# Second block's mixing stage: half of the RWKV mix ahead of the key ranking, half gates moved, key squares and first values on ScalarE

## What is computed

```
h = rms_norm(x)
cols_a, cols_b, gate_a, gate_b = split(h @ w_in)
cols = cols_a + (token_shift(cols_a) - cols_a) * mu     # the RWKV mix; token_shift moves rows down by one
r, k, v, wd, ad, gd = split(cols)                       # 512, 512, 512, 64, 64, 128 columns
a, g = sigmoid(a0 + ad @ a2), sigmoid(gd) @ g2
v_first = v  (layer 0)   or   v = v + (v_first - v) * sigmoid(v0 + (v @ v1) @ v2)  (layer 1)
kk = heads(k * k_k);  kk = kk / max(sqrt(sum(kk * kk)), 1e-12)      # 8 heads of 64
y_a = rwkv7_scan(r, decay, k, v, -kk, kk * a)  (then normed, and times g)
y_b = attention over the 64 keys that rank highest by an index score, from cols_b
x = x + (sigmoid(gate_a) * (y_a @ w_a) + sigmoid(gate_b) * (y_b @ w_b)) @ w_out
```

## Time and profile before

| what | value |
|---|---|
| median of 3 runs | 2837.88 us (2837.84 to 2838.81) |
| profiled execution | 2834.33 us, its span 2832.2 us |
| PE busy | 2696.9 us (95%) |
| DVE busy | 1518.7 us (54%) |
| ACT busy | 1051.0 us (37%) |
| POOL busy | 144.5 us (5%) |
| mean granted TensorE clock | 0.984 |

### The profile page before, as it was taken

The page is one execution under the profiler, slowest core; times in us unless marked ns, Lnnn a source line. Parts: engine busy times, 40 slices in busy tenths (PEclk is TensorE's granted clock), DMA queues, the critical chain, the costliest instruction groups (busy, mean ns, idle before and its releaser), DMA issues.

```text
span 2832.2 us, 35062 instructions
## 1 busy us (share of the span) xinstructions
PE 2696.9 (95%) x15034; PEld 2016.6 (71%) x15034; DVE 1518.7 (54%) x1662; ACT 1051.0 (37%) x1223; POOL 144.5 (5%) x117
## 2 busy tenths in 40 slices
PE   9999999999999999998899999988899899999998
PEld 7886687887878686886565468875564588785477
DVE  5455536455454535456773354457743457564367
ACT  4433434434443333433320144433201245454255
POOL 0002000000021000001011000010110000000000
PEclk9999999999999999998999999999999899999999
DMA  6654235656553254653422435545214167577786
GB/s 238 218 188 149 75 134 193 214 185 218 185 176 131 90 179 157 207 174 139 159 84 75 151 134 206 180 154 159 91 61 148 30 223 265 203 244 246 260 282 230
DMA packets 227470, 483.98 MB, mean 171 GB/s; under 512 B 11676, under 2 KB 45084, under 8 KB 227124
## 3 DMA queue, kind: packets, MB, share of 16 engines
q1 hardware_dynamic: 227316, 481.75, 49.3%
HBM read 477.01 MB, written 2.95 MB: 169 GB/s over the span
## 4 chain that ended last, share of the span: by engine, by line
PE 83%; DVE 11%; ACT 2%; DMA 2%; issue 2%; SPq 0%; POOL 0%; DVEq 0%; POOLq 0%; ACTq 0%
PE psum L424 17%; PE psum L426 17%; PE psum L425 17%; PE psum L427 15%; PE psum L471 4%; DVE weight_ring_low_halves L419 3%; PE psum L3162 2%; PE psum L2301 2%; PE psum L579 2%; PE psum L2387 1%; PE psum L988 1%; ACT weight_high_halves L413 1%; PE psum L681 1%; DMA weight_ring<-in_w_in 1%; PE psum L3092 1%
## 5 line engine op out<-in xcount | busy, mean ns | idle before, releaser
L419 DVE TENSOR_TENSOR weight_ring_low_halves<-weight_ring,weight_high_halves 128x2048 fp32r<-128x2048 f32 (+3 forms) x310 | 684.1, 2211 | 632.7 <-ACT weight_high_halves L413 632.4
L424 PE MATMUL psum<-weight_high_halves,stage_area_halves 128*128 128x512 f32 (+3 forms) x2150 | 827.1, 385 | 20.9 <-ACT stage_area L560 10.0
L426 PE MATMUL psum<-weight_high_halves,stage_area_halves 128*128 128x512 f32 (+3 forms) x2150 | 812.6, 378 | 0.0
L413 ACT ACTIVATE weight_high_halves<-weight_ring 128x2048 fp32r<-128x2048 f32 (+2 forms) x323 | 595.5, 1848 | 565.8 <-PE psum L426 244.8
L425 PE MATMUL psum<-weight_ring_low_halves,stage_area_halves 128*128 128x512 f32 (+2 forms) x1930 | 727.4, 377 | 0.0
L424 PEld LDWEIGHTS psum<-weight_high_halves,stage_area_halves 128*128 128x128 f32 x2150 | 406.5, 189 | 142.0 <-issue 46.1
L427 PE MATMUL psum<-weight_ring,stage_area 128*128 128x512 f32 x1088 | 475.0, 595 | 5.8 <-issue 5.8
L426 PEld LDWEIGHTS psum<-weight_high_halves,stage_area_halves 128*128 128x128 f32 x2150 | 406.4, 189 | 79.7
L425 PEld LDWEIGHTS psum<-weight_ring_low_halves,stage_area_halves 128*128 128x128 f32 x1930 | 364.7, 189 | 68.5 <-issue 0.2
L427 PEld LDWEIGHTS psum<-weight_ring,stage_area 128*128 128x128 f32 x1088 | 205.1, 191 | 257.8 <-issue 257.5
L560 ACT ACTIVATE stage_area<-psum 128x512 f32<-128x512 f32 (+3 forms) x134 | 73.6, 559 | 474.8 <-PE psum L426 148.5
(11 more groups left out here) (312 smaller groups left out, 2455.4 us busy)
## 6 DMA issues: line engine op xcount, KB each, us to landing
weight_ring<-in_ffn_w_gate SPq DMA_DIRECT2D x44, 1024.0 KB, 5.1
weight_ring<-in_ffn_w_up SPq DMA_DIRECT2D x44, 1024.0 KB, 5.2
weight_ring<-in_ffn_w_down SPq DMA_DIRECT2D x44, 1024.0 KB, 5.0
weight_ring<-in_w_in SPq DMA_DIRECT2D x36, 1024.0 KB, 5.3
weight_ring<-in_moe_wd SPq DMA_DIRECT2D x27, 1024.0 KB, 5.0
weight_ring<-in_moe_wu SPq DMA_DIRECT2D x25, 1024.0 KB, 7.1
weight_ring<-in_moe_wg SPq DMA_DIRECT2D x22, 1024.0 KB, 6.1
weight_ring<-in_mem_w_kv SPq DMA_DIRECT2D x16, 1024.0 KB, 5.3
```

Source lines behind the costliest of these rows:

```text
L413: act.raw.activation(self.high_half(name), self.in_slot(name), ACT.Copy).then_inc(*act.mark("high_halves", ("high", name)))
L419: v.raw.tensor_tensor(self.low_half(name), self.in_slot(name), self.high_half(name), ALU.subtract).then_inc(*v.mark("low_halves", ("halves ...
L424: pe.raw.matmul(out, a[1], w[0], start=start, stop=False)
L426: return pe.raw.matmul(out, a[0], w[0], start=False, stop=stop)
```

## The change

The mix is cut in two. Columns of r and k (`mix_first`) are mixed before DVE copies the turned heads, the rest (`mix_rest`) after the attention as before. The DMAs for the shifted r and k rows, and their part of mu, stand in the stream right behind the pieces of `colsA`, ahead of gate (0, 0)'s, and wait for the first two column blocks alone. Both zero rows are cleared by POOL. One row tile of gate (0, 1) is multiplied ahead of the attention, in both layers, and in layer 1 one row tile of gate (1, 1) ahead of the operands' turn; the other row tiles stay where the whole gates were. The squares of kk and their sums move to ACT, as 16 instructions of 64 columns, behind the second sigmoid and ahead of the copies of g; the copy of layer 0's first values moves to ACT behind these copies. The eight parameter rows of RWKV are loaded when the last values are multiplied instead of when they are copied.

```
-        order = [(b, m) for b in range(len(pr["cols"])) for m in range(MT)]
+        order = [(b, m) for b in range(len(pr["cols"])) for m in rows]
...
+        self.mu_rk, self.mu = net.part(12288, D), net.part(18688, N_A - D)
...
             st["a_in"] = net.plan_proj(f"rwkv{l}_in", w[:, 0:N_A], blocks(N_A), KT, split=True)
+            taken = [(st["a_in"]["tag"], "out", b, m) for b in range(2) for m in range(MT)] + self.turn_need(("mix", l))[0] + self.turn_need(("mix", l))[1]
+            net.load_param(("mu_rk", l), self.mu_rk, row_broadcast(ins["rwkv_mu_2"][l][0:D], D), [("x", x0 + 3 * l, 1)])
+            self.load_shifted(l, 0, taken)
...
-            net.load_param(("vec", l, j), self.vec[:, j, :], src, [(f"dsa{l}", "oT", 1)], topic="loaded_rwkv_vectors")
+            net.load_param(("vec", l, j), self.vec[:, j, :], src, [(f"dsa{l}", "weighted", 3)], topic="loaded_rwkv_vectors")
...
+    def zero_gpsimd(self, pool, l, i, taken):
+
+        pool.wait_ge(*pool.at(*taken))
+        pool.raw.memset(self.shifted[i][1][0:1, 0, :], 0.0).then_inc(*pool.mark("zero_row_ready", ("zero_row", l, i)))
...
+    def mix_vector(self, v, l, i):
+        v.wait_ge(*v.at(("loaded", ("shift", l, i, 2)), ("loaded", ("mu" if i else "mu_rk", l)), ("zero_row", l, i)))
+        for event, cols, B, mu in self.mix_rest if i else self.mix_first:
...
         act.raw.activation(self.a, self.a, ACT.Sigmoid).then_inc(*act.mark("rate_sigmoid", ("a", l)))
+        self.key_squares_scalar(act, l)
         for m in range(MT):
             act.wait_ge(*act.at(("wag", l, 2, m)))
...
+        else:
+            act.raw.activation(net.vfirst[:, :].rearrange("p (m n) -> p m n", m=MT), self.v, ACT.Copy).then_inc(*act.mark("first_values_kept", "vfirst"))
...
+    def key_squares_scalar(self, act, l):
+
+        act.wait_ge(*act.at(("keys_scaled", l)))
+        for m in range(MT):
+            for h in range(8):
+                part = slice(h * HD, (h + 1) * HD)
+                inst = act.raw.activation(self.squares[:, m, part], self.kk[:, m, part], ACT.Square, accum_out=self.hs[:, 8 * m + h:8 * m + h + 1])
+        inst.then_inc(*act.mark("keys_squared", ("key_squares", l)))
...
         v.raw.tensor_tensor(self.bh, self.r, self.k, ALU.mult).then_inc(*v.step())
         v.wait_ge(*v.last)
+        v.wait_ge(*v.at(("key_squares", l)))
...
             self.gate_tensor(pe, l, 0, 0)
+            self.gate_tensor(pe, l, 0, 1, [0])
             pairs_tensor(net, pe, f"dsa{l}", self.dsa_heads(l), self.dsa_pairs)
 
-            self.gate_tensor(pe, l, 0, 1)
+            self.gate_tensor(pe, l, 0, 1, [1])
...
             self.gate_tensor(pe, l, 1, 0)
+            self.gate_tensor(pe, l, 1, 1, [0] if l else [])
             net.turn_tensor(pe, self.operand_turn(l))
             self.solve_tensor(pe, l)
             self.chunks_tensor(pe, l)
 
-            self.gate_tensor(pe, l, 1, 1)
+            self.gate_tensor(pe, l, 1, 1, [1] if l else range(MT))
...
             net.split_vector(v, pieces[12:])
+            self.mix_vector(v, l, 0)
             net.turn_copy(v, self.dsa_turn(l))
-            v.wait_ge(*v.at(*net.proj_names(st["a_in"])))
-            v.raw.memset(self.shifted[0][1][0:1, 0, :], 0.0)
-            v.raw.memset(self.shifted[1][1][0:1, 0, :], 0.0).then_inc(*v.mark("zero_row_ready", ("zero_row", l)))
...
-            self.mix_vector(v, l)
+            self.mix_vector(v, l, 1)
```

More of the change, by code:

```diff
@@ L472, in passes, with proj_tensor @@
                 yield i, k, mm
-    def proj_tensor(self, pe, pr, lhsT, bank, need=(), turn_1=(), rows_first=False, before_last=(), before=(None, ())):
+    def proj_tensor(self, pe, pr, lhsT, bank, need=(), turn_1=(), rows_first=False, before_last=(), before=(None, ()), rows=range(MT)):
         tag, kts = pr["tag"], pr["kts"]
         halves = kts // 4
-        order = [(b, m) for b in range(len(pr["cols"])) for m in range(MT)]
+        order = [(b, m) for b in range(len(pr["cols"])) for m in rows]
         if turn_1:
@@ L1765, in __init__ @@
         self.at, self.bh, self.tmp = rows(17408), rows(18432), rows(19456)
+        self.squares = by_m(net.ax_buf[:, 0:D])
         self.vT, self.vv = net.part(17408, 4, S), net.part(20480, S)
@@ L1825, in __init__ @@
                 if (nb, j) == (0, 1):
[L1826 to L1831, removed]
+                    self.load_shifted(l, 1, net.proj_names(st["a_in"]))
+                    net.load_param(("mu", l), self.mu, row_broadcast(ins["rwkv_mu_2"][l][D:N_A], N_A - D), [("dsaT", l, "k")])
                 if (nb, j) == (1, 1):
@@ L1860, in __init__, with load_shifted @@
             self.layers.append(st)
+    def load_shifted(self, l, i, taken):
+        net = self.net
+        cols, to = self.shifted[i]
+        topic = ("loaded_shifted_keys", "loaded_shifted_rest")[i]
+        net.load_param(("shift", l, i, 0), to[1:113], self.colsA[0:112, :, cols], taken, topic=topic)
+        net.load_param(("shift", l, i, 1), to[113:P], self.colsA[112:P - 1, :, cols], topic=topic)
+        net.load_param(("shift", l, i, 2), to[0:1, 1, :], self.colsA[P - 1:P, 0, cols], topic=topic)
     def load_vectors(self, l):
@@ L2183, in prepare_vector @@
         v.wait_ge(*v.at(("loaded", ("vec", l, 7))))
-        v.raw.tensor_tensor(self.kk, self.k, row(2), ALU.mult).then_inc(*v.step())
-        v.wait_ge(*v.last)
+        v.raw.tensor_tensor(self.kk, self.k, row(2), ALU.mult).then_inc(*v.mark("keys_times_factor", ("keys_scaled", l)))
         net.turn_copy(v, self.low_rank_turn(l)[1:])
-        if l == 0:
-            self.key_squares_vector(v, l)
         for j, dst in ((0, self.sig), (1, self.a)):
@@ L2223, in prepare_vector @@
             v.raw.tensor_tensor(self.v, self.v, self.bh, ALU.add).then_inc(*v.step())
-            v.wait_ge(*v.last)
-        else:
-            v.raw.tensor_copy(net.vfirst[:, :].rearrange("p (m n) -> p m n", m=MT), self.v).then_inc(*v.step())
             v.wait_ge(*v.last)
@@ L2553, in gate_bank, with gate_tensor @@
         return 2 if (nb, j) == (0, 0) else 6
-    def gate_tensor(self, pe, l, nb, j):
+    def gate_tensor(self, pe, l, nb, j, rows=range(MT)):
         net = self.net
@@ L2558, in gate_tensor, with gate_scalar @@
         net.proj_tensor(pe, self.layers[l]["gates"][nb, j], lambda k, m: net.xT[:, k, m * P:(m + 1) * P],
-                        lambda b, m: self.gate_bank(nb, j) + m, joined)
-    def gate_scalar(self, act, l, nb, j):
+                        lambda b, m: self.gate_bank(nb, j) + m, joined, rows=rows)
+    def gate_scalar(self, act, l, nb, j, rows=range(MT)):
         net, tag = self.net, self.layers[l]["gates"][nb, j]["tag"]
-        for m in range(MT):
+        for m in rows:
             bank = self.gate_bank(nb, j) + m
@@ L2857, in gpsimd @@
             self.join_gpsimd(pool, l)
+            self.zero_gpsimd(pool, l, 0, [])
             rstd(("dsa", l), 0, 18)
             rstd(("dsai", l), 20, 2)
+            self.zero_gpsimd(pool, l, 1, self.net.proj_names(self.layers[l]["a_in"]))
             rstd(("kk", l), 0, 16)
```

26 lines of the change are left out of this document (9 added, 17 removed).

## The result

| | before | after | ratio |
|---|---|---|---|
| first comparison, four runs each | 2837.86 us (2834.83 to 2838.81) | 2822.34 us (2818.59 to 2828.09) | 0.9946 [0.9931, 0.9962] |
| repeat, on one chip | 2837.56 us (25 runs) | 2827.47 us (6 runs) | 0.9963 [0.9949, 0.9978] |
| second repeat, on another | 2835.91 us (23 runs) | 2827.70 us (12 runs) | 0.9967 [0.9955, 0.9978] |
| all 22 runs after, 87 before | 2837.4 us (2828.4 to 2843.7) | 2827.4 us (2818.6 to 2832.1) | |

Single executions of one kernel lie up to 15 us apart, and their time goes largely with the mean granted clock of TensorE (before: 2829.7 us at 0.985, 2842.2 at 0.981).

What follows compares the result with a forecast made beforehand. PE was taken to bound the kernel (83% of the chain). Terms -0.8 - 8.85 - 1.0 = -10.65 us took the profiled 2834.33 to 2823.7; with 3.55 for the median, 2827.2 us, range 2823.0 to 2833.0.

Steps and rivals of the forecast that it cites:

- more is gained: Rival: ACT's sums cost under 0.37 us each and the clock stays up, giving 2824.2 us; chance 0.15.
- Mix of r and k: Ahead of DVE's turned-head copies: layer 0 hides it at no cost; layer 1's index scores come 0.8 us later.
- The parameter rows: Loads beside the attention's end: between 0 and 2 us late for kk, taken as 0.
- Half ahead of the attention: Half of gate (0, 1) fills PE's pause before the attention: 2.5 us gained in layer 0, 1.7 in layer 1.
- 1.0 for the clock: First turns in both layers: shorter PE idleness may keep the clock up, 0 to 2.3 us together, taken as 1.0.
- Layer 0 behind the attention: Operands' turn starts at 1447.8 instead of 1448.59 us, as ACT's sums give back the earlier start: -0.8 us.
- The row against ScalarE: Squares and sums take DVE 2.5 us, ACT 5.9; leaving them on DVE would gain 1.7 us more in layer 0.
- Layer 1 behind the attention: Operands' turn at full speed saves 2.45 us, half a gate gone behind the scan 7.0; together -8.85 with 0.6 later start.
- Late rows: Rival: shifted rows five us late in both layers delay index and gates, giving 2832.4 us; chance 0.09.
- a loss from the sums on ACT: Rival: each of 16 sums takes 1.06 us, both layers lose, giving 2844.4 us; chance 0.05.
- it does nothing: Rival: the halves push out attention and turn by as much as they save behind; time stays; chance 0.03.
- The clock doesn't follow: Rival: PE stays slow in the pairs and the turn, 1.0 + 2.45 us are missing, giving 2830.7 us; chance 0.11.

Runs made afterwards that it cites:

- g11_whole: The changed kernel with gate (1, 1) whole again behind the scan in both layers; 2826.70 us.
- mix_before: The changed kernel with the mix of r and k back behind the attention and its rows loaded there; 2833.67 us.
- after_again: The changed kernel once more, unedited, giving its third profile; 2827.70 us, ratio 0.9967 to before.
- only_turn: The changed kernel with all undone but layer 1's half of gate (1, 1), the early loads and zero rows on POOL; 2830.91 us, ratio 0.9980 to before.
- halves_whole: The changed kernel with gates (0, 1) and (1, 1) both whole again; 2831.94 us, ratio 0.9986 to before.
- g01_whole: The changed kernel with gate (0, 1) whole again behind the attention in both layers; 2831.85 us.

## Why the prediction was right or wrong

**The sum came out, the range did not.** The sum of -10.65 us met 22 runs after and 87 before at -10.0; that it came out so near is partly luck, as its terms below miss in opposite directions. The step that failed is the one from the profiled execution to the median, with the range around it: the runs' own error was taken as half a microsecond or so, because three runs of before lay within 1 us, and the 3.55 us between the median and the profiled execution were carried over as a constant. The runs scatter by 13 to 15 us, and the profiled execution of after was the highest of its first four: not 3.55 below the median but 5.8 above it (0.2 above and 2.8 below in the two repeats). Of medians of four taken from the 22 runs, 95% lie between 2821 and 2831, so the range needed some 2 us more below, and even then 2822.3 is near its end. The case "more is gained" comes near the first median, but its mechanism is only half there.

**The two layers, step by step.** From PE's first turn of heads to the end of the gate and the merge's first rows behind the scan, from PE's rows: layer 0 took 177.8 and 181.2 us in the two profiles of before and 174.2 in all three of after; layer 1 186.7 and 185.0 before, 183.6, 183.9 and 180.3 after. Means: -5.3 and -3.3, -8.6 together, where the prediction had -1.3 and -9.35 with 0.5 of the clock in each. So the two terms were off in opposite directions.

- *Mix of r and k, layer 0: right.* No wait for rows; the index scores start 3.18 us after PE's first turn of heads, as before. *Layer 1: right*: there it is 4.02, 3.95 and 3.69 us in the three profiles instead of 3.17, so 0.5 to 0.85 later where 0.8 was taken. The parameter rows were taken at 0 for a price of 0.7 us an issue, which is the smallest of the three in the earlier trace rows (707/994/2377 ns); still, DVE waits for them only in some traces, 0.67 us in layer 1 of g11_whole.
- *Half ahead of the attention: right.* DVE waits 3.49 us for the first scores (3.6 worked out), PE 0.78 for bank 7 (0.9), and the low-rank products of layer 0 start 2.73 us earlier, 3.18 counted from PE's turn of the heads (2.5). Undone, it costs 4.4; the prediction had 2.5 + 1.7 + 1.0. Part of the 1.0 for the clock is seen: the first turn of layer 0 takes 2.05 us where it took 2.93 in both profiles of before; in layer 1 it still takes 2.93. The early mix is what lets the half pay: with the mix back behind the attention (mix_before) PE waits for DVE at the low-rank products instead.
- *Layer 0 behind the attention: too small.* The row of 64 columns takes 0.24 us, not 0.37, so ACT is through 16 x 0.13 = 2.1 us sooner than worked out. The operands' turn starts 80.8 us after the index scores; before it was 82.8, and 87.7 in the execution with a slow gate. That is -2.0 in place of -0.8 against the first profile, and the rest of -5.3 is slow clock that the three profiles of after don't have in this layer (1.6 us behind the scan in the first profile of before, 4.9 at sums and gate in the second).
- *The row against ScalarE: wrong.* The prediction held that squares left on VectorE would gain 1.7 more. The wait that this makes is not at the end but at the front: the adds come late, and PE stands 2.03 us for the decay's sigmoid. The row of durations was right and its place was left out. Measured, the two places are alike, 2828.0 and 2827.5 us, with an error of some 3 us that would hide 1.7; in the trace the turn is 0.8 us later and not earlier. The Trainium skill ("ScalarE: Activation LUTs", Rules for kernel authors) puts multiplications on VectorE. No gain by that rule shows in this kernel.
- *Layer 1 behind the attention: right in the rows, but slow clock was left out.* The turn takes 3.66 us without a pause, and the gate behind the scan 20.87 instead of 27.73, as said; in after_again the operands are done 4.6 us before the turn, where 4.8 was worked out. That profile's layer is 6.4 us shorter than the first of before, and it has 2.8 us of slow clock behind the scan; without these it would be 9.2 shorter, an estimate that meets the -9.35.
- *What was not in the sum at all:* that slow clock. In two of three profiles of after, L2182, L2186 and the gates of layer 1 take 2.98 + 3.41 + 23.34 us where the third has 1.98 + 1.84 + 20.85: 5.1 us. In the second profile of before a slow stretch there was paid out of the wait for DVE; with that wait filled it counts in full. The prediction let the clock fall only behind pauses that it knew, and put every other place at nothing.
- *The half of gate (1, 1) is worth less than the 8.85 suggests,* as that term holds all edits together. The half alone brings 6.7 us (only_turn), the mix and the squares without either half 4.0 (halves_whole), both of these together, with gate (0, 1) whole, 6.0 (g01_whole) and not 10.7. The rows give a reason for the missing 4.7, though no run holds it alone: squares off DVE take 2.5 us of the wait of 4.71 and the 2.45 of the slow turn, and the half would have taken the same. Left for it are 2.2 us by the row of halves_whole and 0.5 by that of g11_whole, too little for the runs to tell.

**The rivals.** Late rows, a loss from the sums on ACT and "it does nothing" are ruled out by the rows above. "The clock doesn't follow" is half true: the turn is fast, another place is slow. "More is gained" had the sums right (0.24 us) and the clock wrong.

**What stays open.** Why some of the slow stretches lie elsewhere from one execution of a kernel to the next (the first two profiles of after agree in layer 1, the third does not), and whether the first four runs were low by chance or by their chip.

## What to carry to other kernels

Two edits that fill the same wait are worth it once: undo each alone, since "alone" (6.7 us here) and "undone" (nothing that the runs could tell) can differ as far as this. Before work taken off an engine is credited, look where that engine stands next: 6.9 us of mix ended in a wait for PE, and only the 2.5 us of squares behind that wait brought the operands forward. Work that moves off an engine must be priced at the place where it stood, by what was queued behind it, not only by how long it takes. And before a range is drawn about a median, look at how single executions scatter: three that agree within 1 us came from a kernel whose runs lie up to 15 us apart.

## What the runs showed of the hardware

TensorE's granted clock fell to half (0.50 in the earlier trace rows, 1.2 of 2.4 GHz) at places of which some are common to all executions and others not. The mean over an execution runs from 0.982 to 0.988 in the 14 profiles. In layer 1 the stretch from 1985 to 2012 us had a mean below 1.00 in seven of nine profiles with half a gate between attention and low-rank products, and in one of five with the whole gate there. That is an association, not a shown cause. The two windows (us, PE, PEld, DVE, ACT and POOL busy, PEclk, DMA share, GB/s) are of the first profile of after and of after_again, the same kernel in two executions:

```profile
1995.00:2010.00 15.00, 14.49 (x38) 7.78 (x36) 12.01 (x13) 8.95 (x38) 3.81 (x1) 0.66 0.20 70
```

```profile
1995.00:2010.00 15.00, 15.00 (x47) 7.54 (x48) 13.44 (x15) 7.96 (x24) 3.80 (x1) 1.00 0.20 70
```

PE is busy for 14.5 and 15.0 of 15 us in the two, with the same program, so the work in this stretch alone does not set its clock. Squares with a sum over 64 columns on ScalarE take 0.24 us each from start to start, though one such row shows 0.24 for the square and 0.19 for the read of the sum: they overlap.
